# FFN activations turned by the DMA engines instead of TensorE, in 16-bit halves, for steps 0 to 9 of 11

## The reference

```
def swiglu(x, w_gate, w_up, w_down):
    return (jax.nn.silu(x @ w_gate) * (x @ w_up)) @ w_down

for l in range(DEPTH):                                   # DEPTH = 2
    x = x + 0.5 * swiglu(rmsnorm(x, norm_ffn1[l]), w1_gate[l], w1_up[l], w1_down[l])
    ... differential attention and retention, output projection ...
    x = x + 0.5 * swiglu(rmsnorm(x, norm_ffn2[l]), w2_gate[l], w2_up[l], w2_down[l])
return rmsnorm(x, norm_final)
```

## Time and profile before

| | |
|---|---|
| median of 3 runs | 993.95 us (992.36 to 994.07) |
| span of the profiled execution | 992.8 us |
| its time as a run | not listed; the span is 0.4 us above the fastest run and 1.15 below the median |
| TensorE busy | 965.0 us, 97% of the span |
| VectorE, ScalarE, GpSimd busy | 547.3, 455.8, 39.7 us |
| L792, the FFN transposes | 176 matmuls, 33.5 us busy |

### The profile page before, as it was taken

How to read it: one execution, slowest core, us unless ns; L and a number is a source line. 1 busy time by engine, 2 the same in 40 slices (tenths; PEclk the granted TensorE clock), 3 DMA queues, 4 the chain that set the end, 5 groups by cost and what they waited for, 6 DMA issues and landing times.

```text
span 992.8 us, 12951 instructions
## 1 busy us (share of the span) xinstructions
PE 965.0 (97%) x4512; PEld 796.2 (80%) x4512; DVE 547.3 (55%) x628; ACT 455.8 (46%) x579; POOL 39.7 (4%) x73
## 2 busy tenths in 40 slices
PE   2999999999999999999999999999999999999997
PEld 2888888888888888888878888888888888888885
DVE  3654545565666645454655545456565755454454
ACT  3634344454573534343453434343655554343432
POOL 3400000000010000000000000000001000000000
PEclk9999999999999999999999999999999999999999
DMA  9664646447245655556536655656634645656541
GB/s 251 219 208 160 208 161 206 171 160 241 91 164 170 205 199 172 208 169 211 188 131 214 188 193 175 205 171 210 209 110 165 213 134 189 212 165 207 164 141 43
DMA packets 123179, 178.70 MB, mean 180 GB/s; under 512 B 5664, under 2 KB 95776, under 8 KB 123136
## 3 DMA queue, kind: packets, MB, share of 16 engines
q1 hardware_dynamic: 121808, 173.56, 52.4%
q0 software_dynamic: 1040, 3.54, 1.5%
q10 hardware_dynamic: 288, 1.05, 0.3%
HBM read 177.08 MB, written 1.05 MB: 179 GB/s over the span
## 4 chain that ended last, share of the span: by engine, by line
PE 95%; DMA 1%; ACT 1%; issue 1%; DVE 1%; SPq 0%; ACTq 0%; POOLq 0%; DVEq 0%; POOL 0%
PE gu L722 20%; PE gu L724 20%; PE gu L723 20%; PE acc L724 10%; PE acc L723 10%; PE acc L722 10%; PE tp L792 2%; DMA raw<-in_w_up_dram 1%; PE tp L737 1%; PE tp L840 1%; PE acc L851 1%; PE tp L863 1%; ACT w_hi L294 0%; ACT wide L394 0%; PE acc L863 0%
## 5 line engine op out<-in xcount | busy, mean ns | idle before, releaser
L478 DVE TENSOR_TENSOR w_lo<-raw,w_hi 128x2048 fp32r<-128x2048 f32 (+1 forms) x168 | 376.2, 2243 | 158.5 <-ACT w_hi L294 158.3
L722 PE MATMUL gu<-w_hi,xT_hi 128*128 128x512 f32 x896 | 353.1, 394 | 11.4 <-DVE w_lo L478 11.0
L724 PE MATMUL gu<-w_hi,xT_lo 128*128 128x512 f32 x896 | 350.2, 391 | 0.0
L723 PE MATMUL gu<-w_lo,xT_hi 128*128 128x512 f32 x896 | 349.7, 390 | 0.0
L294 ACT ACTIVATE w_hi<-raw 128x2048 fp32r<-128x2048 f32 (+1 forms) x168 | 313.8, 1872 | 21.8 <-DMA raw<-in_w_up_dram 11.4
L722 PEld LDWEIGHTS gu<-w_hi,xT_hi 128*128 128x128 f32 x896 | 168.8, 188 | 46.7 <-issue 12.3
L336 ACT ACTIVATE hid<-gu,st 128x256 f32<-128x256 f32 x88 | 41.8, 475 | 352.2 <-PE gu L724 352.1
L724 PEld LDWEIGHTS gu<-w_hi,xT_lo 128*128 128x128 f32 x896 | 168.7, 188 | 35.7
L723 PEld LDWEIGHTS gu<-w_lo,xT_hi 128*128 128x128 f32 x896 | 168.9, 189 | 34.1
L722 PE MATMUL acc<-w_hi,aT_hi 128*128 128x512 f32 x384 | 157.0, 409 | 0.0
L534 DVE SCALAR_TENSOR_TENSOR hid<-gu,st,hid 128x256 f32<-128x256 f32 x88 | 42.5, 483 | 205.3 <-ACT hid L336 205.3
(11 more groups left out here) (111 smaller groups left out, 396.4 us busy)
## 6 DMA issues: line engine op xcount, KB each, us to landing
raw<-in_w_gate_dram SPq DMA_DIRECT2D x88, 512.0 KB, 4.0
raw<-in_w_up_dram SPq DMA_DIRECT2D x88, 512.0 KB, 5.0
raw<-in_w_down_dram SPq DMA_DIRECT2D x88, 512.0 KB, 4.3
raw<-in_w_in_dram SPq DMA_DIRECT2D x40, 512.0 KB, 4.6
raw<-in_w_out_dram SPq DMA_DIRECT2D x16, 512.0 KB, 3.7
raw<-in_w_in_dram SPq DMA_DIRECT2D x16, 256.0 KB, 3.0
gain<-in_norm_ffn_dram POOLq DMA_DIRECT2D x3, 512.0 KB, 4.0
gain<-in_norm_mix_dram POOLq DMA_DIRECT2D x2, 512.0 KB, 4.8
```

The lines of the kernel that those rows point to most:

```text
L478: nc.vector.tensor_tensor(w_lo[:, pos % SLOTS, 0:n], raw[:, pos % RAW, 0:n], w_hi[:, pos % SLOTS, 0:n].bitcast(F32), ALU.subtract).then_in ...
L722: nc.tensor.matmul(out_, s_hi, m_hi, start=first, stop=False)
L723: nc.tensor.matmul(out_, s_hi, m_lo, start=False, stop=False)
L724: return nc.tensor.matmul(out_, s_lo, m_hi, start=False, stop=last)
```

## The change

In steps 0 to 9 of every FFN, the tile `hidden` isn't turned by TensorE. GpSimd copies it as 16-bit words, low halves and high halves apart (`turn_out`, into `halves`); ScalarE issues one transposing transfer for each token tile, from SBUF to SBUF (`turn`, into `halvesT`, four blocks of 128x128 words); GpSimd joins the halves again (`turn_back`, into `hidT`); ScalarE and VectorE make `aT_hi` and `aT_lo` from `hidT` in SBUF (`turned_hi`, `turned_lo`). The buffers lie in `kT` and `qT`, which the FFNs don't use. Step 10 keeps the transposes on TensorE (`last_step`, `last_hi`, `last_lo`).

The orders change with it. ScalarE: silu 0, high part of a piece, issue of transfer 0, silu 1, high part, issue of transfer 1, `aT_hi` of tile 0, high part, `aT_hi` of tile 1. VectorE: `hide` 0, low part, `hide` 1, low part, `aT_lo` 0, low part, `aT_lo` 1, and `hide` waits until GpSimd has read the tile of the step before. GpSimd has four copies in each step, in the order out 0, out 1, back 0, back 1; the back-copies wait until VectorE has read the `hidT` of the step before. The copies of step 0 of the first FFN, and the load of the second gain, stand before the tables `bias8` and `decay`; those of step 1 stand behind them. GpSimd's loop over layers is written out.

The diff, cut to its core:

```
@@ -84,6 +85,9 @@
         bias8 = sb("bias8", [P, HEADS, SEQ])
         decay = sb("decay", [P, HEADS, SEQ])
         ident = sb("ident", [P, P])
+        halves = kT[:, 0:2, :].rearrange("p a n -> p (a n)").bitcast(U16).rearrange("p (t h n) -> p t h n", t=TT, h=2)
+        halvesT = kT[:, 2:4, :].rearrange("p a n -> p (a n)").bitcast(U16).rearrange("p (t h n) -> p t h n", t=TT, h=2)
+        hidT = qT[:, 2:4, :]
         lams = qT[:, 0:2, :].rearrange("p a (b n) -> p (a b) n", b=2)
         gsub2 = sb("gsub2", [P, DEPTH, V])
         gsub = sb("gsub", [P, V])
...
@@ -228,6 +235,41 @@
                 pool.wait_ge(head_tmp, 4 * layer + i + 1)
                 nc.gpsimd.tensor_tensor(h_rstd[:, fs], h_tmp[:, fs], neg_half, ALU.pow).then_inc(done, 1)
 
+            def next_gain(q, src):
+                pool.wait_ge(xg_ready, 4 * q + 4)
+                load_gain(src)
+
+            def turn_out(d, e, tt):
+
+                pool.wait_ge(hidden_done, e + 1)
+                pool.sem_inc(pool_seen, 1)
+                nc.gpsimd.tensor_copy(halves[:, tt, :, :], hidden[:, tt, :].bitcast(U16).rearrange("p (n h) -> p h n", h=2)).then_inc(halves_done, 1)
+
+            def turn_back(d, tt):
+
+                pool.wait_ge(halvesT_loaded[tt], 8 * (d - tt) + 16)
+                pool.sem_inc(pool_seen, 1)
+                nc.gpsimd.tensor_copy(hidT[:, tt, :].bitcast(U16).rearrange("p (n h) -> p h n", h=2), halvesT[:, tt, :, :]).then_inc(hidT_done, 1)
+
+            def step(d, e, again=True):
+
+                for tt in range(TT):
+                    turn_out(d + tt, e + tt, tt)
+                for tt in range(TT):
+                    if again:
+                        pool.wait_ge(dT_lo_done, d + tt - 1)
+                    turn_back(d + tt, tt)
+
+            def first_steps(layer, f):
+                i = 2 * layer + f
+                step(2 * (STEPS - 1) * i, 2 * STEPS * i, False)
+
+            def ffn(layer, f):
+                i = 2 * layer + f
+                d0, e0 = 2 * (STEPS - 1) * i, 2 * STEPS * i
+                with pool.Fori(1, STEPS - 1) as s_:
+                    step(2 * s_ + d0, 2 * s_ + e0)
+
             nc.gpsimd.memset(ident[:, :], 0.0).then_inc(pool_steps, 1)
             nc.gpsimd.memset(neg_half, -0.5).then_inc(pool_steps, 1)
             pool.wait_ge(pool_steps, 2)
...
@@ -244,6 +286,8 @@
                 nc.gpsimd.memset(neg_init[:, l:l + 1], -LAM_INIT[l]).then_inc(pool_steps, 1)
             for tt in range(TT):
                 entry(0, tt)
+            next_gain(0, norm_mix[0, :])
+            first_steps(0, 0)
             nc.gpsimd.iota(bias8[:, :, :], pattern=[[0, HEADS], [-1, SEQ]], base=P, channel_multiplier=1,
                            allow_small_or_imprecise_dtypes=True).then_inc(pool_steps, 1)
             pool.wait_ge(pool_steps, 4 + DEPTH)
...
@@ -257,10 +301,6 @@
             nc.gpsimd.affine_select(out=decay[:, :, :], in_=decay[:, :, :], compare_op=ALU.is_ge, fill=0.0, base=0,
                                     pattern=[[0, HEADS], [1, SEQ]], channel_multiplier=-1).then_inc(consts_made, 1)
 
-            def next_gain(q, src):
-                pool.wait_ge(xg_ready, 4 * q + 4)
-                load_gain(src)
-
             def mixer_and_ffn2_entry(layer):
                 for tt in range(TT):
                     entry(3 * layer + 1, tt)
...
@@ -272,16 +312,17 @@
                 for tt in range(TT):
                     entry(3 * layer + 2, tt)
 
-            next_gain(0, norm_mix[0, :])
-            mixer_and_ffn2_entry(0)
-            if DEPTH > 1:
-                with pool.Fori(1, DEPTH) as layer:
-                    next_gain(3 * layer - 1, norm_ffn1[layer, :])
+            for layer in range(DEPTH):
+                if layer:
                     for tt in range(TT):
                         entry(3 * layer, tt)
                     next_gain(3 * layer, norm_mix[layer, :])
-                    mixer_and_ffn2_entry(layer)
-            next_gain(3 * DEPTH - 1, norm_final[:])
+                    first_steps(layer, 0)
+                ffn(layer, 0)
+                mixer_and_ffn2_entry(layer)
+                next_gain(3 * layer + 2, norm_ffn1[layer + 1, :] if layer < DEPTH - 1 else norm_final[:])
+                first_steps(layer, 1)
+                ffn(layer, 1)
             for tt in range(TT):
                 entry(3 * DEPTH, tt)
...
@@ -335,20 +377,42 @@
                         act.wait_ge(slot_free, SLOTS + LP * layer + SLOTS * it + base + pos + 1)
                     nc.scalar.activation(silu_g[:, tt, :], gu[tt][:, 0:CH], ACT.Silu, scale=rstd[:, tt:tt + 1]).then_inc(silu_done, 1)
 
-                def hidden_hi(e, par, tt):
-                    act.wait_ge(hT_psum, e + 1)
+                def turn(d, tt):
+                    act.wait_ge(halves_done, d + 1)
+                    act.sem_inc(halves_seen, 1)
+                    act.dma_start(halvesT[:, tt, :, :].rearrange("p h (k n) -> p (h k) n", k=2),
+                                  halves[:, tt, :, :].rearrange("p h n -> p (h n)"), transpose=True).then_inc(halvesT_loaded[tt], 16)
+
+                def turned_hi(d, par, tt):
+                    act.wait_ge(hidT_done, d + 1)
+                    nc.scalar.activation(aT_hi[:, 2 * par:2 * par + 2, tt * P:(tt + 1) * P],
+                                         hidT[:, tt, :].rearrange("p (k n) -> p k n", k=2), ACT.Copy).then_inc(dT_hi_done, 1)
+
+                def last_hi(par, tt):
+                    act.wait_ge(hT_psum, 2 * i + tt + 1)
                     nc.scalar.activation(aT_hi[:, 2 * par:2 * par + 2, tt * P:(tt + 1) * P],
                                          tp[tt][:, 0:CH].rearrange("p (k n) -> p k n", k=2), ACT.Copy).then_inc(hT_hi_done, 1)
 
-                def step(s_, par, it, pos, nxt):
+                def step(s_, d, par, it, pos, nxt):
+
+                    silu(s_, 0, it, pos)
+                    nxt(0)
+                    turn(d, 0)
+                    silu(s_, 1, it, pos)
+                    nxt(1)
+                    turn(d + 1, 1)
+                    turned_hi(d, par, 0)
+                    nxt(2)
+                    turned_hi(d + 1, par, 1)
+
+                def last_step(s_, par, it, pos, nxt):
 
                     silu(s_, 0, it, pos)
                     nxt(0)
                     silu(s_, 1, it, pos)
-                    hidden_hi(2 * s_, par, 0)
+                    last_hi(par, 0)
                     nxt(1)
-                    hidden_hi(2 * s_ + 1, par, 1)
-                    nxt(2)
+                    last_hi(par, 1)
 
                 def pieces(it, *lots):
...
@@ -526,29 +590,47 @@
                     xT_parts(q, tt)
 
             def ffn(layer, f, base):
-                e0 = 2 * STEPS * (2 * layer + f)
-
-                def hide(e, tt):
+                i = 2 * layer + f
+                e0, d0 = 2 * STEPS * i, 2 * (STEPS - 1) * i
+
+                def hide(e, tt, guard=None):
 
                     dve.wait_ge(silu_done, e + 1)
+                    if guard is not None:
+                        dve.wait_ge(halves_done, guard)
                     nc.vector.scalar_tensor_tensor(hidden[:, tt, :], gu[tt][:, CH:2 * CH], rstd[:, tt:tt + 1], silu_g[:, tt, :],
                                                    ALU.mult, ALU.mult).then_inc(hidden_done, 1)
 
-                def hidden_lo(e, par, tt):
-                    dve.wait_ge(hT_hi_done, e + 1)
+                def turned_lo(d, par, tt):
+                    dve.wait_ge(dT_hi_done, d + 1)
+                    ks = slice(2 * par, 2 * par + 2)
+                    lo_of(aT_lo[:, ks, tt * P:(tt + 1) * P], hidT[:, tt, :].rearrange("p (k n) -> p k n", k=2),
+                          aT_hi[:, ks, tt * P:(tt + 1) * P], dT_lo_done)
+
+                def last_lo(par, tt):
+                    dve.wait_ge(hT_hi_done, 2 * i + tt + 1)
                     ks = slice(2 * par, 2 * par + 2)
                     lo_of(aT_lo[:, ks, tt * P:(tt + 1) * P], tp[tt][:, 0:CH].rearrange("p (k n) -> p k n", k=2),
                           aT_hi[:, ks, tt * P:(tt + 1) * P], hT_lo_done)
 
-                def step(e, par, it, nxt):
-
-                    hide(e, 0)
+                def step(e, d, par, it, nxt, guard=True):
+
+                    hide(e, 0, d - 1 if guard else None)
                     nxt(0)
-                    hide(e + 1, 1)
-                    hidden_lo(e, par, 0)
+                    hide(e + 1, 1, d if guard else None)
                     nxt(1)
-                    hidden_lo(e + 1, par, 1)
+                    turned_lo(d, par, 0)
                     nxt(2)
+                    turned_lo(d + 1, par, 1)
+
+                def last_step(e, d, par, nxt):
+
+                    hide(e, 0, d - 1)
+                    nxt(0)
+                    hide(e + 1, 1, d)
+                    last_lo(par, 0)
+                    nxt(1)
+                    last_lo(par, 1)
 
                 def pieces(it, *lots):
```

(48 more changed lines are left out.)

## The result

The changed kernel takes 986.70 us (median of 4 runs, 986.27 to 986.81), the kernel before 993.44 (median of 4, 992.36 to 994.07): ratio 0.993, 95% interval 0.9916 to 0.9945, 6.7 us faster. 983 was forecast, in a range of 975 to 1045.

The account below looks back on a forecast made before the run. TensorE, busy 965.0 of 992.8 us, was taken as the bound; −17.6 us for removed transposes plus a 7.0 us stall at the start gave 993.95 − 10.6 = 983 us; own range 975 to 990, whole range 975 to 1045.

Parts of the forecast that it names:

- The removal: TensorE, steps 0 to 9 of four FFNs: 80 transpose pairs gone at 0.22 us each, 17.6 us saved.
- The loop hides the new path: FFN loop step: copies, transfers and parts fit beside TensorE's work in 16.39 us; price 0.
- The bound on L: FFN loop: transfer's issue-to-landing time, taken as 4.5 us, stays hidden up to 9.3, or 7.0 if back-copies meet low parts.
- the rival of the latency bound: FFN loop: ScalarE's wait for transferred tiles sets the step in 40 changed steps; 1045 us, chance 0.27.
- The tables on GpSimd's queue: First FFN's start: tables ahead of step 1's copies delay piece 6's low part; TensorE stalls once, 7.0 us.
- The clock: TensorE: taken at the full granted clock, 2.4 GHz; no term for a change of it.
- The other starts: Starts of the other three FFNs: silu 0 of step 1 about 3.6 us late, price 0.
- The estimate of 5.2 us: Transposing transfer: four crossbar blocks in turn take 5.2 us; loop still hides it, sum 0.7 us longer.
- the starts eat the gain: Rival, FFN starts: slow transfers or late weights plus copy meetings cost 24 us; 1000 us, half of it 992; chance 0.11.

Follow-up runs that it names:

- p1: p0 with GpSimd's mask and decay tables moved behind step 9 of the first FFN: 975.35 us, ratio 0.9813.
- p6: p1 with two iotas on GpSimd ahead of tile 1's back-copy in each of steps 0 to 9: 988.78 us, ratio 0.9958.
- p0: Changed kernel with plain transfers in place of the transposing ones, activations not turned: 986.43 us, ratio 0.9929.
- p2: p0 with the tables' iota and four scalings left between steps 0 and 1, the rest behind step 9: 980.75 us, ratio 0.9868.
- p5: p0 with GpSimd's tables ahead of step 0's copies instead of behind them: 975.56 us, ratio 0.9825.
- e3: Kernel before without the transposes of steps 0 to 9 and nothing in their place, activations not turned: 975.77 us, ratio 0.9815.

## Why the prediction was right, and where not

- *The removal.* Forecast 17.6 us for 80 pairs, measured 17.6 alone (975.77). That they agree so well is luck, two errors met: a pair is worth 0.255 in the loop, since the down projection's matmuls also come a little closer, and in that kernel some of it is lost at the layer's turn. In the changed kernel the pairs gave 20.
- *The loop hides the new path.* Right: 16.32 us a step, silu waiting for TensorE. The single prices: GpSimd's copy out takes 0.61 us and the one back 0.77 when alone (forecast 0.9), the issue 1.21 (1.0), the landing 3.1 (4.5). A low part and a copy do meet. VectorE's low part at 140.69 takes 2.47 us where it overlaps the back-copy begun at 140.31, and a copy that starts in a low part took 2.60. That is the exclusion which the Trainium skill states (SBUF — State Buffer, "Who interferes with whom"), and these rows agree with it in both directions, the one that starts second becomes longer. Not every row does: in the kernel before, GpSimd's scaling of `decay` (29.17 to 31.95) and a low part (30.68, 2.29 us) overlap by 1.27 us (by GpSimd's spans, which are rough), and neither is longer than elsewhere.
- *The bound on L.* L = 9.3, or 7.0 with meetings, was too wide. This is the term that the round lacked. The round of the late regime, measured without transposing at 13.9 us with 4.8 us from the issue to the back-copy in it, has two more terms: tile 1's hide waits behind a low part (1.5 us in p1, 49.43 instead of 47.9), and the copy out runs beside one (2.5 us instead of 0.61). Together they put the second issue 3.0 us behind the end of its piece (52.68 against 49.7). So L could grow by 2.4 us, not by 5, before TensorE waits; the changed kernel's own late steps, 14.1 us, say 2.2. The loop was hidden, but with less to spare than the sum said, and the rival of the latency bound was nearer.
- *The tables on GpSimd's queue.* The step that decided, and right in place, cause and order. The size was off: 8.96 us instead of 7.0. The four scalings took 5.56 us instead of 3.44, a low part of VectorE lying in them, and transfer 1 took from 36.59 to about 42.5, 5.9 us instead of 4.5. Tile 1's hide was 1.7 us earlier than forecast, so the chain ended only 0.7 late (61.6 for 60.9). But TensorE was early too: its third projection began at 49.84, not 51.2, and it needed piece 6 at 52.6, not 53.9. With the tables elsewhere the kernel with plain transfers gains 11.1 us.
- *The clock.* Left out, put at nothing without a reason. A standing TensorE came back at half the clock and the stall cost 3.0 us more than it lasted. With it the sum in the forecast's own terms is −17.6 + 8.96 + 3.0 = −5.6, against −6.7 in the medians. By the table it is −20 for the pairs, +12.1 for the stall and −0.4 at the two ends, about the −8.2 of the spans. So the time came out near the forecast because a removal sized 2.4 us too low stood against a stall sized 5.1 too low.
- *The other starts.* 0 forecast. Right in the time (−5.1, −4.8, −5.0 us an FFN); ScalarE does come late there (steps of 12.2 to 15.5 us, mostly 14.1 to 14.5, while it catches up) and TensorE doesn't notice.
- *The estimate of 5.2 us* for the crossbar's four blocks, from the 1309 ns a block of the Trainium skill (VectorE: DVE Perf Modes, "The three transpose paths"), was too high as an addition: the whole transfer lands in 3.1 us, a plain one in 3.0.
- *A slip in the rivals.* Half of the 24 us of "the starts eat the gain" gives 993.95 − 17.6 + 12 = 988, not 992. That lies inside the forecast's own range, so this rival was less apart from the forecast than it reads.

Open: the changed kernel with its transposing transfers and the tables behind step 9 or ahead of step 0 has no run here, and no more has one with a second transposing transfer. That it would take some 976 us is an estimate: it rests on the plain transfers being as fast (986.43 against 986.70), which holds for the whole and not for each stretch. From its own trace, 986.7 less the 12.1 us of stall and half clock, the estimate is 975. Why TensorE stands for 0.2 to 0.8 us at the layer's turn in some kernels and 1.7 to 1.9 in others was not settled either.

## What to carry to other kernels

Work that leaves the bounding engine is gained only if its new path is also short where the pipeline starts, so walk the orders of the prologue as well as the loop, and look for one-off work in the queue that the change makes part of the path. Latency is hidden against the round of the late regime, in which the engines' orders collide, and it must leave room to catch up; the steps right behind a start show that round in the trace. Count a stall of TensorE with the half clock that can follow it: here it added 1.5 to 3.0 us to stands of 2.1 us and more, and to two of five near 1.8 us.

## What was not expected of the hardware

- TensorE's granted clock fell from 2.4 to 1.2 GHz with 8.96 us of standing (15 matmuls at 0.43 us), with 8.36 (7 matmuls), after 3.38 us (8 matmuls, beginning 6 matmuls later), in p6 after 2.40 and 2.09 us (8 and 9 matmuls), and at the layer's turn after 1.94 us in p0 and 1.78 us in p1 (8 matmuls each). At the same place, with the same transposes 5 to 6 us ahead, stands of 1.92, 1.74 and 1.81 us in p2, p5 and e3 left it at 2.4 GHz, and so did 1.45 us in p6. So the length of the stand alone doesn't decide, and the same stall can cost 1.5 or 3.0 us.
- A transposing transfer of 128 x 512 16-bit words from SBUF to SBUF costs 1.21 us to issue and 3.1 to land, against 0.48 and 3.0 for a plain one (medians of 80), though it makes almost four times the packets and takes the engines 6.5% of the span instead of 3.5%.
- GpSimd splits 512 words of 16 bits per partition in 0.61 us and joins them in 0.77, nearer to an iota's speed (1.01 for 1024 elements) than to its float scalings' (0.86 for 256).
